# A head's output with channels on the partitions, and one joint norm product, in a hybrid decoder block

## What is computed

```
o = chunk_gated_delta_rule(l2_normalize(q) * 128**-0.5, l2_normalize(k), v, g, beta)
y_gdn = rms_norm(o, norm_w) * silu(z)          # mean over the head's 128 channels
y = h_lru * gelu(gate)                         # the recurrent half, its own 128 channels
y_rg = rms_norm(y, rg_norm_w)                  # mean over these 128 channels
x = x + concat(y_gdn, y_rg) @ w_out
```

## Time and profile before

| | us |
|---|---|
| median of 3 runs | 1462.7 (1461.94 to 1463.28) |
| profiled execution, its own time | 1460.42 |
| its span, from the first to the last instruction | 1458.6 |
| PE busy in the span | 1337.9 (92%) |
| DVE busy | 632.6 (43%) |
| ACT busy | 442.5 (30%) |
| POOL busy | 64.9 (4%) |

### The profile page before, as it was taken

How to read it: one execution, slowest core, us unless ns; L and a number is a source line. 1 busy time by engine, 2 the same in 40 slices (tenths; PEclk the granted TensorE clock), 3 DMA queues, 4 the chain that set the end, 5 groups by cost and what they waited for, 6 DMA issues and landing times.

```text
span 1458.6 us, 20243 instructions
## 1 busy us (share of the span) xinstructions
PE 1337.9 (92%) x7708; PEld 831.1 (57%) x7708; DVE 632.6 (43%) x1159; ACT 442.5 (30%) x849; POOL 64.9 (4%) x63
## 2 busy tenths in 40 slices
PE   4899999999999999898898999899889889889986
PEld 3899999999988743442353353343343344335332
DVE  5968888888865611231223212212223123221323
ACT  5455656656654411111021011111111111101112
POOL 0012220122110000000000000000000000000000
PEclk9999999999999999999999999999999999999999
DMA  7555555555546869999999999999999999999995
GB/s 204 152 154 155 152 149 153 134 155 150 194 139 216 353 268 428 429 427 428 427 428 429 428 428 429 428 408 421 428 429 426 429 428 426 429 428 428 427 425 242
DMA packets 147649, 481.77 MB, mean 330 GB/s; under 512 B 11449, under 2 KB 113042, under 8 KB 122130
## 3 DMA queue, kind: packets, MB, share of 16 engines
q1 hardware_dynamic: 147602, 481.10, 84.1%
HBM read 478.96 MB, written 2.12 MB: 330 GB/s over the span
## 4 chain that ended last, share of the span: by engine, by line
PE 62%; DMA 29%; DVE 6%; ACT 1%; issue 1%; SPq 1%; DVEq 0%; ACTq 0%
PE bank L595 60%; DMA ew<-in_expert_w_dram 25%; DMA mixT<-in_expert_w_dram 3%; DVE w_parts L1499 1%; PE bank L598 1%; SPq L539 1%; DMA fw<-in_norm_ffn_w_dram 0%; DVE hT L1956 0%; ACT fw_r L1333 0%; DVE ew L1538 0%; DVE ew L1979 0%; DVE fw_r L1819 0%; DVE fw L1459 0%; ACT ew L1410 0%; DVE fw L2022 0%
## 5 line engine op out<-in xcount | busy, mean ns | idle before, releaser
L595 PE MATMUL bank<-ew,hT 128*64 128x512 f32 (+1 forms) x1556 | 464.0, 602 | 63.6 <-DMA ew<-in_expert_w_dram 39.5
L595 PEld LDWEIGHTS bank<-ew,hT 128*64 128x64 f32 (+1 forms) x1556 | 156.9, 141 | 356.4 <-issue 356.1
L595 PE MATMUL bank<-act_parts,w_parts 128*128 128x256 f32 x2304 | 308.5, 288 | 1.7 <-DVE w_parts L1499 1.7
L595 PEld LDWEIGHTS bank<-act_parts,w_parts 128*128 128x128 f32 x2304 | 285.4, 191 | 3.3 <-issue 1.4
L595 PE MATMUL bank<-ew 128*64 128x512 f32 (+2 forms) x1120 | 250.0, 577 | 6.8 <-DVE ew L1981 6.8
L595 PE MATMUL bank<-mixT,hT 128*64 128x512 f32 x512 | 230.7, 605 | 0.0
L1967 DVE TENSOR_TENSOR fw<-fw,bank 128x512 f32<-128x512 f32 x128 | 79.2, 681 | 227.2 <-PE bank L595 227.2
L595 PEld LDWEIGHTS bank<-ew 128*64 128x64 f32 (+1 forms) x1120 | 85.3, 142 | 148.7 <-issue 132.8
L1408 ACT ACTIVATE ew<-bank,gs 128x512 f32<-128x512 f32 x32 | 22.0, 687 | 480.2 <-PE bank L595 480.2
L1499 DVE TENSOR_TENSOR w_parts<-fw,w_parts 128x2048 fp32r<-128x2048 f32 x64 | 147.8, 2313 | 25.8 <-ACT w_parts L1098 24.8
L1428 ACT ACTIVATE ye_r<-bank 64x512 fp32r<-64x512 f32 x128 | 75.7, 591 | 203.9 <-PE bank L595 202.4
(11 more groups left out here) (245 smaller groups left out, 1088.0 us busy)
## 6 DMA issues: line engine op xcount, KB each, us to landing
ew<-in_expert_w_dram SPq DMA_DIRECT2D x157, 2048.0 KB, 17.1
mixT<-in_expert_w_dram SPq DMA_DIRECT2D x32, 2048.0 KB, 19.8
fw<-in_w_in_dram SPq DMA_DIRECT2D x48, 1024.0 KB, 5.8
fw<-in_w_out_dram SPq DMA_DIRECT2D x16, 1024.0 KB, 5.0
ew<-in_expert_w_dram SPq DMA_DIRECT2D x4, 1024.0 KB, 18.1
mixT<-in_x_dram SPq DMA_DIRECT2D x1, 2048.0 KB, 7.7
fw<-in_x_dram SPq DMA_DIRECT2D x1, 2048.0 KB, 9.5
out_dram<-fw SPq DMA_DIRECT2D x4, 512.0 KB, 2.7
```

The costliest lines, as they stand in the source:

```text
L595: return nc.tensor.matmul(o, l, r, start=start, stop=stop, skip_group_check=True)
```

## The change

The output product takes the values as the stationary operand and the attention matrix as the moving one, so o comes out with channels on the partitions. Its squares, with the scaled squares of the query added by POOL (a new `squares` there), stand beside those of the recurrent half in one buffer `sqs` of 128x512. One product with ones sums both. ACT takes two roots of 128x256, DVE one reciprocal of 128x512 (at `between(2)`, now behind the convolution), and `finish` multiplies three times. The query sums, `query_norms`, `scaled` and the transposes `norms` go. ACT's query squares move from the end of a body to level 1. In the last head `square_sums` comes after eight of the 16 steps that are left. The parts of the diff that are left out take away the old buffers and semaphores, add new ones and a third constant (`eps_c[:, 2:3]`), drop the first head's query squares from the prelude, and drop ACT's loop bookkeeping.

```diff
--- before.py
+++ after.py
@@ -199,11 +199,9 @@
         pm = R1b.take(NT, P)
-        on = R1b.take(NT, P)
-        sqy = R1b.take(T)
+        sqs = R1b.take(2, T)
         yb = R1b.take(T)
-        junk1 = R1b.take(P)
         xc = R2.take(T)
...
@@ -646,14 +636,6 @@
-            def query_sums(h):
-
-                pe.wait_ge(s_aa, h + 1)
-                pe.wait_ge(s_sq2, h + 1)
-                for t in range(NT):
-                    l = mm(bank[4][:, T + NT + t:T + NT + t + 1], sq[:, t * P:(t + 1) * P], ones[:, 0:1], True, True)
-                l.then_inc(s_ssm, 1)
-
             def values(h):
@@ -670,17 +652,11 @@
-            def norms(h):
-
-                pe.wait_ge(s_on, h + 1)
-                for t in range(NT):
-                    l = tr(bank[7][:, T + t * P:T + (t + 1) * P], on[:, t, :])
-                l.then_inc(s_oT, 1)
-
             def square_sums(h):
                 pe.wait_ge(s_sqy, h + 1)
-                mm(bank[6][:, 0:T], ones, sqy, True, True).then_inc(s_ssy, 1)
+                pe.wait_ge(s_sqo, h + 1)
+                mm(bank[6][:, :], ones, sqs.rearrange("p b i -> p (b i)"), True, True).then_inc(s_ssy, 1)
@@ -688,11 +664,9 @@
                     pe.wait_ge(s_T, h * (LEVELS - 1) + lv)
-                    if lv == 1:
-                        query_sums(h)
-                        if last_done:
-                            pe.wait_ge(s_ri, h * 2 + 2)
-                            square_sums(h - 1)
+                    if lv == 1 and last_done:
+                        pe.wait_ge(s_ri, h * 2 + 2)
+                        square_sums(h - 1)
                     for t in range(NT):
@@ -709,8 +683,6 @@
                         values(h)
-                    if lv == 3 and last_done:
-                        norms(h - 1)
@@ -720,15 +692,14 @@
                 mm(bank[5][:, P:2 * P], A[:, 1, 1, :], yv[:, 0, :], True, True).then_inc(s_r1m, 1)
-                pe.wait_ge(s_w, h + 1)
-                mm(bank[7][:, 0:P], A[:, 0, 0, :], yv[:, 0, :], True, True)
-                mm(bank[7][:, P:T], A[:, 0, 1, :], yv[:, 0, :], False, False)
+                pe.wait_ge(s_aq, h + 1)
+                mm(bank[7][:, 0:T], yv[:, 0, :], A[:, 0, 0:2, :].rearrange("p t i -> p (t i)"), True, False)
                 fill(4)
                 pe.wait_ge(s_r1, h + 1)
                 mm(bank[5][:, 2 * P:3 * P], tt[:, 1, 1, :], yv[:, 1, :], True, True).then_inc(s_y1m, 1)
                 fill(4)
                 pe.wait_ge(s_y1, h + 1)
-                mm(bank[7][:, P:T], A[:, 0, 2, :], yv[:, 2, :], False, True).then_inc(s_o, 1)
+                mm(bank[7][:, P:T], yv[:, 2, :], A[:, 0, 2, :], False, True).then_inc(s_o, 1)
                 fill(8)
@@ -796,10 +767,11 @@
             heads(NH - 1, fill_w, True, None)
+            for _ in range(8):
+                next(steps)
             square_sums(NH - 1)
             for _ in steps:
                 pass
-            norms(NH - 1)
             pe.wait_ge(s_mixLP, 2)
@@ -1122,8 +1094,7 @@
-                act.wait_ge(s_silu, h * 3 + 2)
-                act.activation(sq, cq[:, 0, :], ACT.Square).then_inc(s_sq2, 1)
+                act.activation(sq, cq[:, 0, :], ACT.Square, scale=(4.0 * HD * EPS) ** 0.5).then_inc(s_sq2, 1)
@@ -1135,25 +1106,14 @@
                 act.wait_ge(s_o, h + 1)
-                for t in range(NT):
-                    l = act.activation(junk1, bank[7][:, t * P:(t + 1) * P], ACT.Square, accum_out=oss[:, t:t + 1])
-                    link(l)
+                act.activation(sqs[:, 0], bank[7][:, 0:T], ACT.Square, scale=QSCALE).then_inc(s_oss, 1)
             def roots(h):
-                act.wait_ge(s_w, h + 1)
-                for t in range(NT):
-                    l = act.activation(fr[:, t:t + 1], oss[:, t:t + 1], ACT.Sqrt, scale=1.0 / HD, bias=cqc[:, t:t + 1])
+                act.wait_ge(s_ssy, h + 1)
+                for b, bias in ((0, 2), (1, 0)):
+                    l = act.activation(sqs[:, b], bank[6][:, b * T:(b + 1) * T], ACT.Sqrt, bias=eps_c[:, bias:bias + 1])
                 l.then_inc(s_rt, 1)
-                act.wait_ge(s_ssy, h + 1)
-                act.activation(sqy, bank[6][:, 0:T], ACT.Sqrt, bias=eps_c[:, 0:1]).then_inc(s_yrt, 1)
-
-            def scaled(h):
-
-                act.wait_ge(s_f, h + 1)
-                for t in range(NT):
-                    l = act.activation(on[:, t, :], bank[7][:, t * P:(t + 1) * P], ACT.Copy, scale=fi[:, t:t + 1])
-                l.then_inc(s_on, 1)
@@ -1194,7 +1154,7 @@
                 act.wait_ge(s_y, h + 1)
-                act.activation(sqy, yb, ACT.Square, scale=0.5 * QSCALE).then_inc(s_sqy, 1)
+                act.activation(sqs[:, 1], yb, ACT.Square, scale=0.5 * QSCALE).then_inc(s_sqy, 1)
...
@@ -1234,6 +1192,9 @@
                         factors(h)
+                        if not first:
+                            act.wait_ge(s_sqo, h)
+                        squares(h)
                         high(h * 6 + 8, 2, h * 2 + 3, (1,))
@@ -1242,8 +1203,6 @@
                         values(h)
-                        if not first:
-                            scaled(h - 1)
                         high(i * 6 + 3, 0, i * 2 + 2)
@@ -1258,7 +1217,6 @@
                     elif n == 8:
-                        squares(i)
                         evac(i, 3)
...
@@ -1596,17 +1553,15 @@
                 dve.wait_ge(s_rt, h + 1)
-                V.reciprocal(fi[:, :], fr[:, :]).then_inc(s_f, 1)
+                V.reciprocal(sqs, sqs).then_inc(s_f, 1)
+                dve.wait_ge(s_f, h + 1)
             def finish(h, rgn):
-                dve.wait_ge(s_oT, h + 1)
-                V.scalar_tensor_tensor(mixT[:, h, :], bank[7][:, T:], gnw[:, 0:1], sz, ALU.mult, ALU.mult)\
-                    .then_inc(s_mix, 1)
-                dve.wait_ge(s_yrt, h + 1)
-                V.reciprocal(sqy, sqy).then_inc(s_yr, 1)
-                dve.wait_ge(s_yr, h + 1)
-                V.scalar_tensor_tensor(mixT[:, h + NH, :], yb, rgn, sqy, ALU.mult, ALU.mult).then_inc(s_mix, 1)
+                V.scalar_tensor_tensor(sqs[:, 0], sqs[:, 0], gnw[:, 0:1], sz, ALU.mult, ALU.mult).then_inc(s_g0, 1)
+                V.scalar_tensor_tensor(mixT[:, h + NH, :], yb, rgn, sqs[:, 1], ALU.mult, ALU.mult).then_inc(s_mix, 1)
+                dve.wait_ge(s_g0, h + 1)
+                V.tensor_tensor(mixT[:, h, :], bank[7][:, 0:T], sqs[:, 0], ALU.mult).then_inc(s_mix, 1)
                 dve.wait_ge(s_mix, h * 2 + 2)
@@ -1629,12 +1584,6 @@
                 dve.wait_ge(s_aq, h + 1)
-
-            def query_norms(h):
-                dve.wait_ge(s_ssm, h + 1)
-                V.tensor_scalar(cqc[:, :], bank[4][:, T + NT:T + 2 * NT], 4.0 * HD * EPS, 16.0 * HD * EPS * EPS,
-                                ALU.mult, ALU.add).then_inc(s_w, 1)
-                dve.wait_ge(s_w, h + 1)
@@ -1706,10 +1655,9 @@
                         params(i)
+                        conv(i, 0)
                         if not first:
                             invert(h - 1)
-                        query_norms(h)
-                        conv(i, 0)
                     elif n == 3:
@@ -1780,9 +1728,8 @@
                 elif n == 2:
+                    add_early(0)
                     invert(h - 1)
-                    query_norms(h)
-                    add_early(0)
                 elif n == 3:
@@ -2041,12 +1988,20 @@
+            def squares(h):
+
+                pool.wait_ge(s_oss, h + 1)
+                pool.wait_ge(s_sq2, h + 1)
+                G.tensor_tensor(sqs[:, 0], sqs[:, 0], sq, ALU.add).then_inc(s_sqo, 1)
+
             decay_mask(0)
             G.tensor_copy(tri_one[:, :], cst[:, C_TRI:C_TRI + 2 * P]).then_inc(s_tri, 1)
             with pool.Fori(0, NH - 1) as i:
                 heads(i)
                 decay_mask(i + 1)
+                squares(i)
             heads(NH - 1)
+            squares(NH - 1)
             for n, lo, hi in ((3, 4, 7), (4, 12, 15)):
```

More of the change, by code:

```diff
@@ L227, in build @@
         wk = sb("wk", [P, NT])
-        cqc = sb("cqc", [P, NT])
         rk = sb("rk", [P, NT])
         sdk = sb("sdk", [P, NT])
-        oss = sb("oss", [P, NT])
-        fr = sb("fr", [P, NT])
-        fi = sb("fi", [P, NT])
         rgp = sb("rgp", [P, 1])
-        eps_c = sb("eps_c", [P, 2])
+        eps_c = sb("eps_c", [P, 3])
         stat = sb("stat", [P, 8])
@@ L357, in build @@
         s_sq2 = sem("s_sq2")
-        s_ssm = sem("s_ssm")
         s_vT = sem("s_vT")
@@ L361, in build @@
         s_D = sem("s_D")
-        s_w = sem("s_w")
         s_aq = sem("s_aq")
@@ L382, in build @@
         s_rt = sem("s_rt")
-        s_yrt = sem("s_yrt")
-        s_yr = sem("s_yr")
+        s_sqo = sem("s_sqo")
+        s_g0 = sem("s_g0")
         s_f = sem("s_f")
-        s_on = sem("s_on")
-        s_oT = sem("s_oT")
         s_ph = sem("s_ph")
@@ L1221, in _ @@
                     tanh_half(0, b - 1)
-            squares(0)
             act.wait_ge(s_prm, 2)
@@ L1226, in _ @@
             gates(0)
-            PER = 2
```

(4 more changed lines are left out.)

## The result

| | us |
|---|---|
| before, median of 6 runs | 1462.99 (1461.94 to 1465.31) |
| after, median of 6 runs | 1470.52 (1468.31 to 1474.71) |
| ratio, 95% interval | 1.0052 (1.0042 to 1.0062) |
| profiled execution after, its own time; span | 1470.90; 1469.1 |
| forecast | 1471.0, range 1463.5 to 1474.0 |

The account below looks back on a forecast made before the run. PE alone was taken to bound the heads, with DVE's short turns able to make it wait. The terms -0.37 - 0.9 + 5.2 + 2.1 - 0.4 + 2.65 gave +8.3 us on the median 1462.7, so 1471.0, range 1463.5 to 1474.

Parts of the forecast that it names:

- the bodies' stall: Bodies 2 to 6: PE waits 1.04 us each before P of level 4 for the reciprocal at `between(2)`, 5.2 in all.
- Body 7: Same wait before level 4, longer as DVE's convolution is later and ACT's moved squares add 0.3: 2.1 us.
- PE's own saving: PE's work falls by 0.15 us in each of bodies 2 to 7, -0.9 in all, and 0.37 in body 1.
- The last head's levels: Last head: reciprocal late for level 3, `finish` 1.3 us shorter before the 1.52 us gap; -0.4 us taken.
- The tail: End of last head: later `square_sums` exposes roots, reciprocal, `rest_out(8)` and `add_early(3)`; PE stands 3.0 us, costing +2.65.
- The clock: Rival, chance 0.12: the tail's 3.0 us gap halves PE's clock behind it, about 1.4 us more, so 1472.4.
- Sum: Whole kernel: all terms together make it 8.3 us slower, 1471.0 on the median.
- the bodies' stalls are hidden: Rival, chance 0.14: a reciprocal under about 2.3 us leaves only body 7 stalling, 1.1 us; 1464.8.
- the tail is hidden: Rival, chance 0.11: work still queued on PE covers DVE's chain at the end of the last head; 1468.3.
- POOL's addition: One 128x256 addition per body in POOL's idle time, counted as nothing; if late, about 1 us at most.

Follow-up runs that it names:

- the dose: Changed kernel with one more 128x128 reciprocal, its result unused, at `between(2)` of bodies 2 to 7: 1477.65 against 1462.99 before the change.
- Undoing the order: Changed kernel with `square_sums` ahead of the 16 steps again in the last head: 1467.74 against 1463.37 before the change.
- three other kernels with this gap: Changed kernel with the 128x512 reciprocal ahead of the convolution (1472.66), with an added 128x128 reciprocal (1477.65), or with its reciprocal moved to level 4 (1469.18).
- The second measurement: The changed kernel unedited, measured again on another chip: 1472.05 against 1462.89 before the change (1.0068).
- the split: Changed kernel with the reciprocal as two 128x256 halves, at `between(2)` and at the start of `finish`: 1463.42 against 1463.37 before the change.
- the placing was undone: Changed kernel with split reciprocal, `square_sums` ahead of the 16 steps, `add_early(1)` ahead of `recur`: 1459.76; kernel before with only that last swap: 1461.25.
- The small matmuls: Changed kernel with 24 unread 128x256 bf16 matmuls in the tail's gap on PE: 1471.53, then 1471.61 beside the changed kernel's 1472.05.

## Why the prediction was right

- **The chain and the bodies' stall.** Forecast 1.04 us for bodies 2 to 6, measured 1.03 (45.83 - 44.80). The line through 2 and 256 elements gave 3.33 us for the reciprocal; it took 3.34. What hid work on DVE in this turn was its idle time in brackets and the distance to PE's due time; both were used up, since the dose cost 0.8 of its 0.86 us. The bodies are 45.83 us apart and not 45.95, as PE saves more than forecast.
- **Body 7.** Forecast 2.1, measured 1.84 in brackets, and 2.0 by the starts: 365.64 - 361.77 is 3.87, where 1.87 is usual. The later convolution and ACT's moved squares did add up there. Before its next `rest` DVE now idles 0.37 us for ACT's `high` (356.67 in its timeline), and before the change it didn't.
- **PE's own saving.** Forecast 0.15 per body, measured 0.25. The mis-sized term is the product with ones: +0.43 by the forecast, while the wide one goes from 258.13 to 258.99, 0.86, where the narrow one took 0.51, so +0.35. The output product saved almost nothing, 0.03 (2.08 from 103.74 to 105.82, before 2.11), as taken.
- **The last head's levels.** Forecast -0.4 from between -1.3 and +0.3; PE resumes at 424.89 where it was 419.28, so +5.6 after +6.1 at level 4 (413.49 in PE's timeline, where the row before the change stood at 407.37): -0.5.
- **The tail.** Forecast +2.65 and a gap of 3.0; 452.76 - 444.76 is 8.0, after 5.6 at the gap before: +2.4, and the gap is 2.56. Undoing the order gave back 1.75 of it in the trace. The rest is the longer product (0.35) and a wait of 1.03 where it was 0.76.
- **The clock.** Given 0.12; both profiles of the changed kernel show it behind the tail's gap, and of three other kernels with this gap two do. As a part of the median it stays unsettled; as an event the chance of 0.12 was too low. The bodies' gaps of 0.8 us left the clock alone, as forecast; body 7's did so in five of six profiles, and not with the dose, where it was 2.67.
- **Sum.** At 452.76 the profiled execution was 8.0 us behind that of before, the forecast 8.3; the clock added 1.6 (471.58 against 462.00). At the experts' first product it is 10.1 (522.61 against 512.53), at the end 10.5. In the medians it is 7.5, because the profiled execution of before was 2.6 us faster than its kernel's median, and that of the changed kernel 0.4 slower. One execution says little about the end: from the experts' first product on, the thirteen profiles take 946 to 951 us.
- **What was luck.** The second measurement gave 9.2 us. Between 7.5 and 9.2 the forecast of 8.3 stands well, but part of that is errors that cancel: PE saved 0.1 more per body and the tail lost 0.25 less than forecast, and the clock cost up to 1.6 that the sum didn't hold.
- **The rivals.** That the bodies' stalls are hidden fell with the profile after, the split and the dose; that the tail is hidden fell with the tail's order undone. POOL's addition takes 0.97 us, as bounded, and no wait of PE is for it. The shown cause is the length of one instruction in one turn of DVE: moved to level 4, the same instruction makes PE wait before level 6.

## What to carry to other kernels

An engine that is busy 84% beside a saturated one has its room in turns, not in the mean: before joining two operations into one wide one, compare its length with the idle time of the very turn that it lands in, plus the slack of the consumer. In bodies 2 to 6 two halves in two turns cost nothing where one whole cost 1.0 us per body. And a chain that ends in another engine's wait is priced from its start: moving its first link eight steps later moved its end past PE's last covered matmul. Joining work for the busy engine was right (0.25 us per body); it paid only once the placing was undone, and then by 0.7 us in the traces and 1.5 in the medians.

## What was not expected of the hardware

- The reciprocal on DVE is linear in the row over the whole width: 0.17 us for 2 elements, 0.95 for 128, 1.74 for 256, 3.34 for 512, so 6.2 ns per element from the shortest to the longest.
- A float32 product costs differently by its neighbours. The product with ones takes 0.51 us for 256 columns and 0.86 for 512, from its start to the next. In a row of two, 256 columns took 0.34 each. So no run here shows that one wide product is cheaper than two narrow ones.
- The clock behind a gap of PE is no function of its length alone. The gap of 1.84 to 1.86 us in body 7 had 1.2 GHz behind it in one of six profiles. That of 1.86 or 1.87 in the last head had it in two of two, that of 2.55 to 2.59 in the tail in four of five. Those in bodies 2 to 6 never had it, 0.8 to 0.9 us each and 1.6 with the dose. Neither had that of 1.52 before the change, nor those of about 1.0 in the last head and its tail.
- A profile shows one execution, and a slow stretch that is gone at one place can come back at another. The small matmuls took 1.7 us off the 72 matmuls behind them; their second profile lost 1.5 of that in body 7, and the medians differ by 0.4, inside the noise.
